# Spreading row fetches and dot products over a decoder trunk's expert layer

## The reference

```python
def peer(xb):                       # xb: normalized tokens
    q = (xb @ w_query).reshape(-1, 8, 2, 128)
    sc = einsum('thpc,hpkc->thpk', q, sub_keys)           # 128 keys, two halves, 8 heads
    s1, i1 = top_k(sc[:, :, 0], 16); s2, i2 = top_k(sc[:, :, 1], 16)
    cand = (s1[..., :, None] + s2[..., None, :]).reshape(-1, 8, 256)
    top, ci = top_k(cand, 16)
    idx = take(i1, ci // 16) * 128 + take(i2, ci % 16)    # 128 experts of 16384 per token
    g = softmax(top)
    hid = gelu(einsum('td,thkd->thk', xb, expert_down[idx]))
    return einsum('thk,thkd->td', g * hid, expert_up[idx])
```

## Time and profile before

| what | us |
|---|---|
| median of three runs | 3507.97 |
| profiled execution | 3483.54 |
| its span | 3481.6 |
| PE busy | 3338.9 (96%) |
| DVE busy | 1871.8 (54%) |
| ACT busy | 1387.1 (40%) |
| POOL busy | 1927.1 (55%) |
| DMA, mean over the span | 232 GB/s |

### The profile page before, as it was taken

The page is one execution under the profiler, slowest core; times in us unless marked ns, Lnnn a source line. Parts: engine busy times, 40 slices in busy tenths (PEclk is TensorE's granted clock), DMA queues, the critical chain, the costliest instruction groups (busy, mean ns, idle before and its releaser), DMA issues.

```text
span 3481.6 us, 47799 instructions
## 1 busy us (share of the span) xinstructions
PE 3338.9 (96%) x18808; PEld 3042.5 (87%) x18808; DVE 1871.8 (54%) x3786; ACT 1387.1 (40%) x2420; POOL 1927.1 (55%) x1071
## 2 busy tenths in 40 slices
PE   7998899998999999999999999999999989999999
PEld 6756789998989889889978878999998989989998
DVE  4534138978885544444422311799589744444443
ACT  3344223337774333333333322333577733333332
POOL 3402347777777455555444644577777763555553
PEclk9978899999999999999989999999999999999999
DMA  2200226558999888888722222466699988888884
GB/s 106 97 13 25 73 92 218 196 196 324 354 372 384 303 307 309 318 325 308 273 85 92 84 91 74 140 210 217 211 375 371 358 331 308 319 308 320 322 310 165
DMA packets 234301, 808.20 MB, mean 232 GB/s; under 512 B 21088, under 2 KB 70240, under 8 KB 225376
## 3 DMA queue, kind: packets, MB, share of 16 engines
q1 hardware_dynamic: 160352, 536.69, 43.0%
q0 software_dynamic: 73728, 268.47, 20.2%
HBM read 702.32 MB, written 102.76 MB: 231 GB/s over the span
## 4 chain that ended last, share of the span: by engine, by line
PE 82%; DMA 7%; DVE 4%; POOL 3%; ACT 2%; issue 1%; SPq 0%; DVEq 0%; ACTq 0%
PE banks L233 22%; PE banks L234 22%; PE banks L235 22%; PE banks L952 3%; DMA hid_scratch<-arena 2%; DMA arena<-down,side 2%; PE banks L916 2%; DMA gathered_rows<-down,side 2%; POOL weights_lo L213 1%; PE banks L248 1%; PE banks L249 1%; PE banks L250 1%; PE banks L280 1%; DVE operand_hi L1080 1%; PE banks L491 1%
## 5 line engine op out<-in xcount | busy, mean ns | idle before, releaser
L213 POOL TENSOR_TENSOR weights_lo<-raw_ring,weights_hi 128x1024 fp32r<-128x1024 f32 x498 | 1287.0, 2586 | 1085.2 <-ACT weights_hi L207 1084.0
L233 PE MATMUL banks<-operand_hi,weights_hi 128*128 128x384 f32 (+1 forms) x4800 | 1676.7, 349 | 35.8 <-ACT arena L810 23.5
L234 PE MATMUL banks<-operand_lo,weights_hi 128*128 128x384 f32 (+1 forms) x4800 | 1649.6, 344 | 0.0
L235 PE MATMUL banks<-operand_hi,weights_lo 128*128 128x384 f32 (+1 forms) x4800 | 1648.9, 344 | 0.0
L233 PEld LDWEIGHTS banks<-operand_hi,weights_hi 128*128 128x128 f32 x4800 | 906.9, 189 | 125.9 <-issue 59.0
L234 PEld LDWEIGHTS banks<-operand_lo,weights_hi 128*128 128x128 f32 x4800 | 906.8, 189 | 29.3 <-issue 3.6
L235 PEld LDWEIGHTS banks<-operand_hi,weights_lo 128*128 128x128 f32 x4800 | 905.7, 189 | 28.3
L207 ACT CAST weights_hi<-raw_ring 128x1024 fp32r<-128x1024 f32 x624 | 652.9, 1047 | 673.9 <-PE banks L235 577.0
L1116 DVE TENSOR_TENSOR residual<-residual,banks 128x384 f32<-128x384 f32 x256 | 141.8, 554 | 650.7 <-PE banks L235 641.2
L810 ACT ACTIVATE arena<-banks 128x384 f32<-128x384 f32 x256 | 125.9, 492 | 531.5 <-PE banks L235 489.4
L782 ACT ACTIVATE arena<-operand_hi,side 128x128 f32<-128x128 f32 x768 | 235.2, 392 | 83.6 <-DVE operand_hi L1080 79.2
(11 more groups left out here) (174 smaller groups left out, 2793.8 us busy)
## 6 DMA issues: line engine op xcount, KB each, us to landing
raw_ring<-weight_tiles SPq DMA_DIRECT2D x624, 512.0 KB
hid_scratch<-arena SPq DMA_DIRECT2D x64, 768.0 KB
gate_scratch<-arena SPq DMA_DIRECT2D x24, 2048.0 KB
arena<-hid_scratch SPq DMA_DIRECT2D x32, 1536.0 KB
arena<-gate_scratch SPq DMA_DIRECT2D x32, 1536.0 KB
arena<-up,side POOLq DMA_INDIRECT x146
residual<-x_t SPq DMA_DIRECT2D x2, 1024.0 KB, 6.8
arena<-key_t SPq DMA_DIRECT2D x2, 1024.0 KB, 5.1
```

Of the source, the lines that this page charges most:

```text
L213: eng.tensor_tensor(wl[:, b, :], raw[:, n % RING, :], wh[:, b, :].bitcast(F32), ALU.subtract).then_inc(done, 1)
L233: pe.matmul(out, w_hi, x_hi[:, c, :], start=start and c == 0, stop=False)
L234: pe.matmul(out, w_hi, x_lo[:, c, :], start=False, stop=False)
L235: last = pe.matmul(out, w_lo, x_hi[:, c, :], start=False, stop=stop and c == DC - 1)
```

## The change

The 128 dot products of a layer and their fetches are placed anew: 42 during the ranking of blocks 1 to 3 (before 12), 54 with the units (before 96), 12 in the last down tiles, and 20 in the first ten up tiles, two each (before 20 behind the units, none in the up tiles). The units and the turn begin three tiles later. The dot products' results are used later: GELU at up tile 11 (before 0), and the quads run from up tile 18 to 114 (before 12 to 123). The last addition of the rows moves from the end to up tile 119. In `route` the call `between()`, at which dot products are put in, stands behind 17 steps of the ranking (before behind 4); the diff is cut there.

```diff
-        UNIT_FROM = 70
+        UNIT_FROM = 73
         UNIT_TILE = [UNIT_FROM + u * 7 // 8 for u in range(UNITS)]
         TURN_TILE = UNIT_FROM - 3
-        EARLY_DOTS = 12
+        ROUTE_DOTS, UNIT_DOTS, TAIL_DOTS = 42, 54, 12
-        QUAD_TILE = [12 + q * 36 // 10 for q in range(QUADS)]
+        QUAD_TILE = [18 + q * 31 // 10 for q in range(QUADS)]
+        W_TILE = 11
...
-        GATHER_DOWN_AT = [17 + k for k in range(DOWN_RING)]
-        GATHER_DOWN_AT += [36 + (k - 6) % 4 + (k - 6) // 4 * 16 for k in range(6, 6 + EARLY_DOTS)]
...
+        def dot_tile(k):
+
+            if k < ROUTE_DOTS:
+                return 19 + k * 51 // ROUTE_DOTS
+            k -= ROUTE_DOTS
+            if k < UNIT_DOTS:
+                return UNIT_TILE[k * UNITS // UNIT_DOTS]
+            k -= UNIT_DOTS
+            if k < TAIL_DOTS:
+                return UNIT_TILE[-1] + 1 + k
+            return PDOWN + (k - TAIL_DOTS) // 2
+
+        GATHER_DOWN_AT = [17 + k // 2 if k < DOWN_RING else dot_tile(k - DOWN_RING) + 1 for k in range(P)]
+        UP_ORDER = [6] + [(P - DOWN_RING + i) % DOWN_RING for i in range(DOWN_RING)]
-        GATHER_UP_AT = [PDOWN - 3 + j for j in range(UP_RING)]
+        GATHER_UP_AT = [PDOWN - 4] + [dot_tile(P - DOWN_RING + i) + 1 for i in range(DOWN_RING)]
...
                 ahead_hi(act, n0 + PQ + PDOWN + v)
-                if v == 0:
+                if v == W_TILE:
                     act.wait_ge(s.dotted, was["dotted"] + P)
...
-                if v == 8:
+                if v == W_TILE + 4:
                     act.wait_ge(s.w_turned, was["w_turned"] + 1)
...
-                if v == PUP - 3:
+                if v == QUAD_TILE[-1] + 2:
                     act.wait_ge(s.quads, was["quads"] + QUADS)
...
             def gather_up(j):
...
-                if j == 1:
-                    pool.wait_ge(s.dotted, was["dotted"] + P)
+                if 1 <= j < UP_RING:
+                    pool.wait_ge(s.dotted, was["dotted"] + P - DOWN_RING + j)
...
                 columns_step(pe, u0 + v, ps[:, v % 4, 0:TD], up_hi[g % 2], up_lo[g % 2],
...
-                if v == 5:
+                if v == W_TILE + 3:
                     pe.wait_ge(s.w_made, was["w_made"] + 1)
...
-                if v == PUP - 2:
+                if v == QUAD_TILE[-1] + 3:
                     pe.wait_ge(s.acc_copied, was["acc_copied"] + 1)
...
+            def route_dots():
+
+                points[0] += 1
+                dot_until(ROUTE_DOTS * points[0] // (3 * 17))
...
             for tt in range(1, TT):
-                route(tt, dot)
+                route(tt, route_dots)
...
-                dot()
-                dot()
-            while dots[0] < P:
-                dot()
+                dot_until(ROUTE_DOTS + UNIT_DOTS * (u + 1) // UNITS)
+            dot_until(ROUTE_DOTS + UNIT_DOTS + TAIL_DOTS // 2)
...
             for j in range(GROUP):
                 gate_slice(0, j)
+            dot_until(ROUTE_DOTS + UNIT_DOTS + TAIL_DOTS)
...
             for v in range(PUP):
                 g, k = v // 8, v % 8
+                dot_until(min(P, ROUTE_DOTS + UNIT_DOTS + TAIL_DOTS + 2 * v + 2))
                 if v + AHEAD < PUP and LO_ON_DVE[u0 + v + AHEAD]:
                     split_lo(dve, u0 + v + AHEAD, lo_dve)
-                if v == 2:
+                if v == W_TILE + 1:
...
+                if v == QUAD_TILE[-1] + 5:
+                    for half in range(2):
+                        dve.wait_ge(s.acc_turned, was["acc_turned"] + half + 1)
```

More of the change, by code:

```diff
@@ L999, in peer_dve, with dot_until @@
             i16 = iota[:, None, None, 0:TOPK].to_broadcast([P, PH, TOPK, TOPK])
+            def dot_until(n):
+                while dots[0] < n:
+                    dot()
             def route(tt, between):
@@ L1005, in route @@
                 link(last)
+                between()
                 for hp in range(2 * PH):
@@ L1118, in peer_dve @@
                     gated_lo(g + 1, k)
-            for half in range(2):
-                dve.wait_ge(s.acc_turned, was["acc_turned"] + half + 1)
-                dve.tensor_tensor(xt[:, 4 * half:4 * half + 4, 0:G], xt[:, 4 * half:4 * half + 4, 0:G],
-                                  ps[:, (7, 4)[half], :].rearrange("p (c t) -> p c t", c=4), ALU.add).then_inc(s.rows_added, 1)
         sv = arena[:, 0:8192].rearrange("p (t v) -> p t v", t=TT)
```

16 lines of the change are left out of this document (10 added, 6 removed).

## The result

The changed kernel takes 3477.02 us (median of 8 runs, 3469.19 to 3484.25), the kernel before in the same job 3509.19 us (8 runs, 3490.22 to 3518.28). The ratio is 0.9913, 95% interval 0.9898 to 0.9927: 32 us gained where 51 were forecast (49 of the profiled execution). The sign and the range hold; the size does not, and 3477 lies 19 us from the forecast's 3458 and 11 from rival (B)'s 3488. The profiled execution of after took 3475.13 us (span 3473.3).

A forecast was written before the change was run, and what follows sets the result against it. DVE's queue and row traffic together were taken to bound the unit stretch. Units -64, ranking +17, tail -4, first up tiles +8, ends -6.3 gave -49 us: 3434, times 1.007 = 3458; likeliest range 3430 to 3480, all 3415 to 3495.

The forecast's parts named there:

- rival (B): Unit stretch stays partly starved by loads, or POOL's long issues push the ranking to its bound; -20, 3488 us, chance 0.14.
- Units: Down tiles with units: fewer dot products and row fetches win 32 us per layer, -64 in all.
- DMA share: Sign in the unit stretch: DMA share below 0.93, from 0.96 before.
- Rival (C): Unit stretch is bound by something that stays, perhaps ACT's chain, and gives nothing; +15, 3523 us, chance 0.09.
- Ranking: Before the turn: 30 more dot products per layer delay the ranking; cost 10 + 7.5 = 17 us.
- The line of failure: Forecast is wrong if the unit stretch stays above 280 us or the ranking costs over 15 in a layer.
- Tail: Last down tiles: weights wait behind the later gate store; 12 us lost for 14.3, 2 us won per layer.
- First up tiles: First ten up tiles: 20 new dot products put DVE above PE's pace; cost 4 us per layer, bounds 0 and 8.
- Ends: Layer ends: the last row addition leaves them, saving 1.90 us in layer 0 and 4.4 in layer 1; together 6.3.
- Rival (A): Unit stretch is won, dot products fit, nothing is paid and the tail loses 5 only; -89, 3418 us, chance 0.15.

The follow-up runs named there:

- e12: Changed kernel with 6 dot products in the ranking instead of 42 and 90 with the units instead of 54; 3484.25 us.
- e2: Changed kernel with the ranking's row fetches, from the seventh on, issued three POOL passes later, dot products unmoved; 3478.82 us.
- e8: Changed kernel with 18 dot products in the ranking instead of 42 and 78 with the units instead of 54; 3445.62 us.
- e1: Changed kernel with 30 dot products in the ranking instead of 42 and 66 with the units instead of 54; 3452.03 us.
- e3: Changed kernel with no dot product in the ranking's first four places, the 42 spread over the other 47, fetch passes moved to fit; 3453.73 us.
- e5: Changed kernel with each up tile's two dot products on DVE moved behind the gates' product instead of ahead of it; 3478.30 us.
- e4: Changed kernel with the low halves of up tiles 3, 5, 7, 9 and 11 made by POOL instead of DVE; 3496.54 us.
- e10: Changed kernel with 30 dot products in ranking, 78 with units, 12 in tail, 8 among up tiles, SP's first gate loads in pass 124; 3427.91 us.
- e11: Changed kernel with 34 later-starting dot products in ranking, 78 with units, 4 among up tiles, SP's first gate loads in pass 124; 3421.29 us.
- e7: Changed kernel with the last addition of the fetched rows back behind the last up tile in both layers; 3493.53 us.
- e9: The kernel before, unchanged, profiled once more; 3506.81 us.

## Why the prediction was right and where it failed

**Units: right.** -66 for -64. Fewer dot products and row fetches a unit took the loss away, and e12 brings part of it back; that the fetches' longer lead had no share in it is not shown. DMA share (0.91 and 0.90 for "below 0.93") and length (261.7 for 261 to 264) as said. Rival (C), that something which stays bounds the units, is out: ACT's 216.6 us are the same in both kernels. Rival (B)'s starved units did not come either. Its other half did in number, +26 for the ranking against +32 measured, and so the total lies nearer to it; but POOL's long issues were not the cause, since e2 gives POOL three passes more and loses the same. But the prediction could not tell how far one may go, and the change went further than the units need: 1.625 a unit costs nothing (e8), and the 24 dot products put into the ranking beyond that bought only loss.

**Ranking: right mechanism, mis-sized.** The term was +17, from "752.36 + 30 x 1.2 + 7.5 = 796" and a layer 1 of 7.5. Measured +32. What was missing in both layers is the 9.1 us by which comparisons and multiplications lengthen (34.2 and 30.4 us in layer 1 too). The first wait came 2.0 us shorter than forecast in layer 0 (14.84 for 16.8) and as forecast in layer 1 (14.72 for 7.24 + 7.5). So layer 0 is 10 + 9.1 - 2.0 = 17.1 for 17.0 measured, and layer 1 7.5 + 9.1 = 16.6 for 15.9. That it closes to a tenth in layer 0 is luck: the ranking ended 6.0 us later than forecast and not 7.7 (9.1 - 2.0 + 0.6), and the last subtractions took 2.90 us for 1.88. The line of failure that the prediction drew, over 15 in a layer, was crossed; e1, e2, e3 and e8 show that it was crossed by DVE's chain.

**Tail: right mechanism, too cautious.** Two estimates stood there, 24 us late (times as in the earlier trace rows) and 2 us (times halved by the lighter traffic), and the middle was taken. SP's queue, ACT and PE, layer 0, after:

```profile
1106.52 0.52 SPq L728 DMA_DIRECT2D gate_scratch<-arena  x1
...
1118.00 0.80 SPq L738 DMA_DIRECT2D arena<-gate_scratch  x2
```

```profile
1136.03 1.04 ACT L207 CAST weights_hi<-raw_ring 128x1024 fp32r<-128x1024 f32 x1 [10.71 <-DMA raw_ring<-weight_tiles]
```

```profile
1140.05 0.69 PE L233 MATMUL banks<-operand_hi,weights_hi 128*128 128x384 f32 x1 [6.95 <-ACT arena L821]
```

Store to gate loads is 11.5 us for 18.8 (forecast by halving: 9.8), and from these to the weights 18.0 for 26.8 (14). Together 29.5 us for 45.6: three quarters of what the traffic argument promised (23.8), and the middle threw half of it away. PE idles 6.95 us at tile 122, not 8 to 14.

**First up tiles: the step that failed.** The prediction let DVE begin late, saw that it "cannot catch up", and charged 4 us a layer with 8 as the bound. It cost 11.1 and 8.8. DVE and then PE, layer 0, after:

```profile
1180.22 0.56 DVE L1123 TENSOR_TENSOR arena<-arena 128x384 f32<-128x384 f32 x1 [8.76 <-DMA arena<-hid_scratch]
...
1198.37 1.22 DVE L1007 CUSTOM_DVE_ANT_0 gathered_rows<-gathered_rows,banks 128x1024 f32<-128x1024 f32 x1 [1.97 <-DMA gathered_rows<-down,side]
...
1201.19 1.22 DVE L1007 CUSTOM_DVE_ANT_0 arena<-arena,banks 128x1024 f32<-128x1024 f32 x1 [1.60 <-DMA arena<-down,side]
```

```profile
1185.44 0.69 PE L233 MATMUL banks<-operand_hi,weights_hi 128*128 128x384 f32 x1 [4.92 <-DVE weights_lo L213]
...
1208.17 0.41 PE L233 MATMUL banks<-operand_hi,weights_hi 128*128 128x384 f32 x1 [4.33 <-DVE weights_lo L213]
```

DVE begins 13.0 us into the stretch, and its addition of tile 0 is 9.3 us behind PE's grid (8.6 before). From there to the addition of tile 9 DVE is busy 41.5 of 46.8 us, 4.6 a tile (forecast 4.4), and idle for 5.3, 4.1 of it for rows, which had no term. So the additions are 18.6 us late at tile 9, and 15.3 at tile 12. Before, at 2.04 us a tile, that lateness fell from 8.6 to 4.0 by up tile 4. What was wrong is the sum: the prediction charged what DVE's pace exceeds PE's by, 0.2 us a tile, and little for the backlog that DVE had worked off before and now could not. e5 (order) and e4 (another engine) did not help; only fewer dot products did (e10, e11). e10 shows the backlog itself: its two layers have the same work, their additions are 10.6 and 13.5 us late at tile 0, and they lose 9.4 and 12.2.

**Ends: right**, 7.6 us by e7 for 6.3; between the two profiled executions 9.2 were read. The stretch between the layers varies by 3 us in itself, more than the 1.6 by which the two differ. Rival (A) had the units right and the tail nearly (8 to 9 us lost, not 5) and was wrong in that nothing would be paid.

**The total: in part luck.** The ranking and the first up tiles cost 27 us more than forecast, and units, tail and ends gave some 10 to 12 us more. The total kept within the narrower range of 3430 to 3480 by 3 us because these offset each other in part.

## What to carry to other kernels

When work is moved out of a stretch, find first how little must go: here 18 of 96 dot products would have done where 42 were moved, and the other 24 bought nothing in the units and cost 16 us a layer in the ranking (e8). An engine with a deadline (DVE before the turn) has to be priced with its instructions as long as they get beside the new neighbour, not as long as they were. And where an engine starts late, compare its pace with that of the one that waits for it: here a start 12.4 us late cost 4.2 at 2.04 us a tile, and one 13.0 us late cost 15.3 at 4.6.

## What the runs showed that was not expected

Attention, which the change does not touch, differs from one execution to the next. The first trace of before, in the dense part of layer 0's attention:

```profile
150.00:250.00 100.00, 98.27 (x390) 63.72 (x388) 29.21 (x116) 39.30 (x98) 19.54 (x10) 0.81 0.13 43
250.00:350.00 100.00, 86.60 (x412) 64.12 (x411) 49.23 (x179) 43.49 (x113) 19.63 (x11) 0.86 0.08 26
```

and e9, the same kernel:

```profile
150.00:250.00 100.00, 97.95 (x333) 62.92 (x332) 23.51 (x94) 33.00 (x81) 18.13 (x9) 0.69 0.13 43
250.00:350.00 100.00, 86.61 (x357) 55.29 (x356) 51.92 (x194) 45.19 (x127) 8.12 (x7) 0.71 0.00 1
```

PE is as busy in both, but the granted clock is 0.69 and 0.71 for 0.81 and 0.86, and PE issues 333 matmuls for 390 in 100 us. The first down tile starts at 520.6 for 495.6: 25 us, most of the size of the change's effect, and not due to it (520 to 527 in all traces but the first). Of eleven more executions of the kernel before, timed together with e9, three took 3468 to 3484 us with a mean granted clock of 0.970 to 0.976, the others 3501 to 3516 with 0.961 to 0.965; in which stretch they differ is not recorded. Two spans alone, 3473.3 and 3481.6, would have shown 8 us. Why the clock differs stays open.

A pause costs PE more than its length. In the ranking 10.8 us of idle go with 17 us of loss, and in the kernel before 22.6 with 34; the granted clock is 0.98 and 0.97 in those stretches where it is 1.00 without pauses. As an estimate from these rows, 0.02 of 321 us is 6 us and 0.03 of 294 is 9, so the clock can account for most of the rest (6 and 11); it was not separated.
